# Moving the running sums into the final banks, and the down biases into the twelfth pair, of a mixture-of-experts stage

## The reference

```python
gu = xb @ w_gate_up[e] + b_gate_up[e]                 # 1024 -> 2048
x_glu = jnp.minimum(gu[:, :D_EXPERT], SWIGLU_LIMIT)
x_lin = jnp.clip(gu[:, D_EXPERT:], -SWIGLU_LIMIT, SWIGLU_LIMIT)
act = x_glu * jax.nn.sigmoid(SWIGLU_ALPHA * x_glu) * (x_lin + 1.0)
yr = act @ w_down[e] + b_down[e]                      # 1024 -> 1024
y = segment_sum(yr * gate, token)                     # over the 4 experts of a token
...
x = x + gt2 * rms_norm(y, g_ffn_post)
```

## Time and profile before

| | us |
|---|---|
| median of 3 runs | 1356.5 |
| lowest and highest of them | 1350.71, 1359.32 |
| the profiled execution | 1350.96 |
| its span, first to last instruction | 1349.3 |
| PE busy in it | 1280.7 |
| DVE, ACT busy | 361.6, 218.8 |
| DMA, mean over the span | 365 GB/s |

### The profile page before, as it was taken

How to read it: one execution, slowest core, us unless ns; L and a number is a source line. 1 busy time by engine, 2 the same in 40 slices (tenths; PEclk the granted TensorE clock), 3 DMA queues, 4 the chain that set the end, 5 groups by cost and what they waited for, 6 DMA issues and landing times.

```text
span 1349.3 us, 15432 instructions
## 1 busy us (share of the span) xinstructions
PE 1280.7 (95%) x6118; PEld 542.0 (40%) x6118; DVE 361.6 (27%) x757; ACT 218.8 (16%) x500; POOL 46.7 (3%) x95
## 2 busy tenths in 40 slices
PE   5999999999999999999999999999999999999996
PEld 2566466665453333333233233223423323342322
DVE  2541325776552121111212102121210212121122
ACT  2124424422220111011011011101101101110101
POOL 1100003010100000000000000000000000000000
PEclk9899999999999999999999999999999999999999
DMA  9847569589878999999999999999999999999992
GB/s 347 276 145 286 192 244 254 175 250 292 313 297 349 408 395 431 428 427 426 426 428 428 428 427 428 427 426 427 428 428 428 426 428 428 428 428 428 429 426 106
DMA packets 72718, 492.25 MB, mean 365 GB/s; under 512 B 12229, under 2 KB 25405, under 8 KB 44868
## 3 DMA queue, kind: packets, MB, share of 16 engines
q1 hardware_dynamic: 68708, 480.99, 88.0%
q0 software_dynamic: 3936, 10.21, 2.6%
HBM read 485.86 MB, written 5.32 MB: 364 GB/s over the span
## 4 chain that ended last, share of the span: by engine, by line
PE 72%; DMA 24%; DVE 2%; issue 1%; ACT 0%; SPq 0%; DVEq 0%; ACTq 0%
PE bank L1987 23%; DMA ring<-in_w_gate_up_dram 22%; PE bank L2014 10%; PE bank L1682 8%; PE bank L1709 5%; PE bank L1975 4%; PE bank L1945 4%; PE bank L1548 2%; PE bank L1670 2%; PE bank L1821 2%; PE bank L1622 2%; PE bank L1998 2%; DMA ring<-in_w_down_dram 2%; PE bank L1949 1%; PE bank L1796 1%; PE bank L1978 1%
## 5 line engine op out<-in xcount | busy, mean ns | idle before, releaser
L1987 PE MATMUL bank<-ring,hga 128*64 128x512 f32 x1024 | 236.7, 599 | 13.1 <-DMA ring<-in_w_gate_up_dram 13.1
L1987 PE MATMUL bank<-ring,work 128*64 128x512 f32 x992 | 229.5, 599 | 13.0 <-DMA ring<-in_w_gate_up_dram 9.3
L2014 PE MATMUL bank<-ring,work 128*64 128x512 f32 x1024 | 228.8, 597 | 8.6 <-DMA ring<-in_w_down_dram 8.5
L2014 PEld LDWEIGHTS bank<-ring,work 128*64 128x64 f32 x1024 | 73.1, 138 | 159.2 <-issue 140.6
L1987 PEld LDWEIGHTS bank<-ring,hga 128*64 128x64 f32 x1024 | 67.3, 136 | 158.4 <-issue 129.1
L1987 PEld LDWEIGHTS bank<-ring,work 128*64 128x64 f32 x992 | 65.1, 136 | 153.8 <-issue 127.9
L1459 DVE TENSOR_SCALAR work<-bank 128x512 f32<-128x512 f32 x32 | 22.1, 692 | 351.7 <-PE bank L1987 351.7
L1682 PE MATMUL bank<-hga,ring 128*128 128x320 f32 x384 | 108.1, 443 | 2.2 <-DVE hga L963 2.2
L877 ACT ACTIVATE work<-bank 64x512 f32<-64x512 f32 x60 | 35.5, 591 | 335.7 <-PE bank L2014 335.0
L1682 PEld LDWEIGHTS bank<-hga,ring 128*128 128x128 f32 x384 | 74.1, 194 | 36.8 <-issue 6.6
L1471 DVE TENSOR_TENSOR gbT<-gbT,bank 128x512 f32<-128x512 f32 x80 | 55.0, 687 | 115.4 <-PE bank L1975 80.0
(11 more groups left out here) (368 smaller groups left out, 872.1 us busy)
## 6 DMA issues: line engine op xcount, KB each, us to landing
ring<-in_w_gate_up_dram SPq DMA_DIRECT2D x126, 2048.0 KB, 22.3
ring<-in_w_down_dram SPq DMA_DIRECT2D x64, 2048.0 KB, 23.2
ring<-in_w_ada_dram SPq DMA_DIRECT2D x12, 2048.0 KB, 10.3
ring<-in_w_in_dram SPq DMA_DIRECT2D x12, 2048.0 KB, 11.2
ring<-in_cache_k_dram SPq DMA_DIRECT2D x64, 128.0 KB, 7.2
ring<-in_cache_v_dram SPq DMA_DIRECT2D x16, 512.0 KB, 8.7
ring<-in_w_out_dram SPq DMA_DIRECT2D x2, 2048.0 KB, 9.7
out_dram<-tok POOLq DMA_DIRECT2D x2, 1024.0 KB, 8.4
```

Of the source, the lines that this page charges most:

```text
L1987: last = mm(B[x + 2 * q][CAP * h:CAP * h + CAP, :], slots[:, k, CAP * x:CAP * x + CAP], units[k // 2][:, k % 2, 1024 * q + 512 * h:1024 * ...
L2014: last = mm(B[4 + y][CAP * j:CAP * j + CAP, :], actT[:, 4 * y + m, CAP * h:CAP * h + CAP], slot[:, m, 512 * j:512 * j + 512], start=(h == ...
```

## The change

1. **Last pair.** `summed` for pieces 0, 1, 2 and 3 moves into x = 0, ahead of and between the two halves of `down(t, 0, ...)` (expert 29); piece 4 follows after k = 1 of x = 1. Pair 14 is combined straight on top of them (`combine_ahead`), so its five pieces are no longer added by DVE. `biases` of x = 1 opens the banks ahead of its eight steps. `SUM_BANK` gets other banks; expert 30's down output and the activations of expert 31 go through B[1] for it. `combine_of(0)` is split: pieces 0, 1 and 4 ahead of the last half of `down`, pieces 2 and 3 after it.
2. **Down biases.** They leave the opening. In pair 12 PE turns the gate weights after k = 1 of x = 0 and combines the biases after k = 4, 5 and 6 of x = 0 (`combine_biases`); DVE copies the gate weights (`gates_out`) and adds the five pieces between its two `acts`. On POOL the memsets of `C` and `Ysb` are gone, and b_down is loaded later, behind the wait for `h2tok_made` and ahead of the four loads of `bgu`.
3. **Loops.** `LOOPED = 8`: the hardware loop covers pairs 1 to 8, and pairs 9 to 14 are written out, on every engine.
4. **The end.** DVE's `post_normed` runs in the order 1, 0, 3, 4, 2 and waits for a square only for 0, 4 and 2; ACT's squares of pieces 1 and 3 wait for DVE instead. There is one root instead of two, and the five `y_out` follow it in one go.

```diff
-        SUM_BANK = [B[7], B[0], B[2], B[3], B[6]]
+        SUM_BANK = [B[7], B[6], B[0], B[2], B[5]]
...
-                with eng.Fori(0, (PAIRS - 4) // unroll) as i:
+                with eng.Fori(0, LOOPED // unroll) as i:
...
-                for u in range(1, 3):
-                    pair(t(PAIRS - 4 + u), PAIRS - 4 + u, u)
+                for i in range(LOOPED + 1, PAIRS - 1):
+                    pair(t(i), i, i % 4, i)
...
-            eng.memset(C, 0.0).then_inc(s["moe_zeroed"], 1)
-            eng.memset(Ysb, 0.0).then_inc(s["moe_zeroed"], 1)
-            eng.wait_ge(s["moe_zeroed"], 3)
-            eng.dma_start(Ysb[0:E, :], b_down[0]).then_inc(s["late_in"], 16)
             eng.wait_ge(s["h2tok_made"], 4)
+            eng.dma_start(bd, b_down[0]).then_inc(s["late_in"], 16)
...
             for k, i in enumerate(SUMMED):
                 eng.wait_ge(s["last_ps"], NPC * n + k + 1)
+                if i in (1, 3):
+                    eng.wait_ge(s["u_made"], 5 + (i + 1) // 2 + i // 2)
...
-                if i == 4:
-                    root(r3[:, 0:2], 8)
-            root(r3[:, 2:3], 9)
+            root(r3, 8)
...
+            def gates_out(t):
+                eng.wait_ge(s["wt_ps"], t + PAIRS - BIASED)
+                V_.tensor_copy(cb[:, 0:SP_], B[7][0:E, SP_:2 * SP_]).then_inc(s["wt_made"], PAIRS // 2)
+                V_.tensor_copy(cb[:, SP_:T], B[7][0:E, 0:NS]).then_inc(s["wt_made"], PAIRS // 2)
...
                 acts(t, 0)
                 experts(i)
+                if at == BIASED:
+                    gates_out(t)
+                    for n in range(NPC):
+                        combined(t - 1, n)
                 acts(t, 1)
...
+            for i, last, squared in ((1, 2, 0), (0, 0, 1), (3, 5, 0), (4, 0, 3), (2, 0, 4)):
+                if last:
+                    eng.wait_ge(s["last_ps"], NPC * n + last)
+                if squared:
+                    eng.wait_ge(s["f_sq"], squared)
+                post_normed(i)
...
+                        if at == BIASED and (x, k) == (0, 1):
+                            eng.wait_ge(s["C_made"], t)
+                            weights_turned()
+                        if at == BIASED and x == 0 and k in (4, 5, 6):
+                            combine_biases(t, ((0, 1), (2, 3), (4,))[k - 4])
...
                 for x in range(2):
                     e = 2 * t + x
+                    if x:
+                        biases(t, x, opens=True)
...
-                        gate_up(x, k, slots_of(3), gu_slot)
-                        if x == 1 and k in (1, 2, 3):
-                            if k == 1:
-                                eng.wait_ge(s["C_made"], t + 2)
-                            combine(t, ((0, 1), (2, 3), (4,))[k - 1])
+                        gate_up(x, k, slots_of(3), gu_slot, opened=(x == 1))
+                        if (x, k) == (1, 1):
+                            eng.wait_ge(s["Y_made"], 2 * t)
+                            summed(4)
+                        if x == 1 and k in (2, 3):
+                            combine_ahead(((0, 1, 2), (3, 4))[k - 2])
...
                     if x == 0:
-                        for h in range(2):
-                            down(t, 0, h, dn_slot[h])
-                summed(4)
-                summed(0)
+                        eng.wait_ge(s["C_made"], t + 1)
+                        summed(0)
+                        summed(1)
+                        down(t, 0, 0, dn_slot[0])
+                        eng.wait_ge(s["lin_made"], 4 * t + 1)
+                        summed(2)
+                        summed(3)
+                        down(t, 0, 1, dn_slot[1])
                 down(t, 1, 0, dn_slot[0])
-                acts_turned(2 * t + 2, 1)
-                summed(3)
+                acts_turned(2 * t + 2, 1, B[1])
                 down(t, 1, 1, dn_slot[1])
-                down(t + 1, 0, 0, dn_slot[2])
-                combine_of(0)
-                down(t + 1, 0, 1, dn_slot[3])
-                combine_of(1)
+                down(t + 1, 0, 0, dn_slot[2], B[1])
+                combine_of(0, (0, 1, 4))
+                down(t + 1, 0, 1, dn_slot[3], B[1])
+                combine_of(0, (2, 3))
+                combine_of(1, SUMMED)
```

More of the change, by code:

```diff
@@ L881, in Y_out, with acts @@
                         link.later(ins)
-            def acts(t, x):
+            def acts(t, x, bank=None):
                 y = 1 - x
@@ L919, in last_pair @@
                     eng.wait_ge(s["dn_used"], 4 * t + 2 + 2 * x)
-                    A_(Ysb[:, 512 * x:512 * x + 512], B[4 + x][:, :], ACT.Copy).then_inc(s["Y_made"], 1)
+                    A_(Ysb[:, 512 * x:512 * x + 512], B[1 if x else 4][:, :], ACT.Copy).then_inc(s["Y_made"], 1)
             def again(r):
@@ L1446, in _ @@
             select(4)
[L1447 removed]
+            eng.wait_ge(s["moe_zeroed"], 1)
             def experts(i):
@@ L1507, in again, with post_normed @@
                 select(2 * PAIRS * r + 4)
-            moe_rounds(eng, first, pair, last_pair, first, again)
+            n = moe_rounds(eng, first, pair, last_pair, first, again)
             eng.wait_ge(s["G3_in"], 48)
-            def post_normed(k):
-                i = SUMMED[k]
-                eng.wait_ge(s["f_sq"], k + 1)
-                link.later(TTo(piece(gbf, i).rearrange("p (t n) -> p t n", t=2), SUM_BANK[i][:, :].rearrange("p (t n) -> p t n", t=2),
-                               G3(2 if i == 4 else i % 2), ALU.mult))
+            def post_normed(i):
+                TTo(piece(gbf, i).rearrange("p (t n) -> p t n", t=2), SUM_BANK[i][:, :].rearrange("p (t n) -> p t n", t=2),
+                    G3(2 if i == 4 else i % 2), ALU.mult).then_inc(s["u_made"], 1)
             def y_out(i):
@@ L1988, in gate_up, with biases @@
                                   units[k // 2][:, k % 2, 1024 * q + 512 * h:1024 * q + 512 * h + 512],
-                                  start=(k == 0), stop=(k == NT - 1))
+                                  start=(k == 0 and not opened), stop=(k == NT - 1))
                 if k % 2:
                     last.then_inc(s["gu_used"], 1)
-            def biases(t, x):
+            def biases(t, x, opens=False):
                 eng.wait_ge(s["esel_made"], t + 1)
@@ L1998, in biases, with acts_turned, down @@
                         mm(B[x + 2 * q][CAP * h:CAP * h + CAP, :], esel[E * j:E * j + E, CAP * x:CAP * x + CAP],
-                           bgu[E * j:E * j + E, :], start=False, stop=False)
-            def acts_turned(e, y):
+                           bgu[E * j:E * j + E, :], start=opens, stop=False)
+            def acts_turned(e, y, bank=None):
                 eng.wait_ge(s["act_made"], e)
                 for m in range(4):
-                    last = tr(B[4 + y][:, SL * m:SL * m + SL], glu[:, half_columns(y, m)], 128)
+                    last = tr((bank or B[4 + y])[:, SL * m:SL * m + SL], glu[:, half_columns(y, m)], 128)
                 last.then_inc(s["aT_ps"], 1)
-            def down(t, x, h, slot):
+            def down(t, x, h, slot, bank=None):
                 y = 1 - x
+                bank = bank or B[4 + y]
                 if h == 0:
@@ L2098, in summed, with combine_ahead, combine_of @@
                     mm(SUM_BANK[i][:, :], ident[:, :], piece(gbf, i), start=True, stop=False)
-                def combine_of(x):
-                    eng.wait_ge(s["Y_made"], 2 * t + 2 + x)
-                    for i in SUMMED:
+                def combine_ahead(pieces):
+                    for n in pieces:
+                        i = SCATTER[n]
+                        k = i // 2
+                        if k < 2:
+                            last = mm(SUM_BANK[i][:, :], C[:, 128 * k:128 * k + 128], Ysb[:, 512 * (i % 2):512 * (i % 2) + 512],
+                                      start=False, stop=False)
+                        else:
+                            for h in range(2):
+                                last = mm(SUM_BANK[i][64 * h:64 * h + 64, :], C[:, SP_:T], Ysb[:, 512 * h:512 * h + 512],
+                                          start=False, stop=False)
+                        last.then_inc(s["scatter_ps"], 1)
+                def combine_of(x, of):
+                    eng.wait_ge(s["Y_made"], 2 * t + 1 + x)
+                    for i in of:
                         k, j = i // 2, i % 2
```

124 lines of the change are left out of this document (55 added, 69 removed).

## The result

| | before | changed |
|---|---|---|
| median of the runs, us | 1357.91 (4 runs, 1350.71 to 1359.91) | 1343.85 (4 runs, 1342.12 to 1345.94) |
| ratio, 95% interval | | 0.9915 (0.9886 to 0.9945) |
| the profiled execution, us | 1350.96 | 1342.12 |
| its span | 1349.3 | 1340.3 |

The change saves 0.85%, with an interval of 0.55 to 1.14%. A second set of 7 runs of the changed kernel, beside 12 of the one before, gave 0.9933 (0.9909 to 0.9958). The two medians of the table differ by more, 14.1 us or 1.04%; the ratio on record is not their quotient (0.9896), which lies inside its interval. Forecast was 0.9926, and 1346.5 us with a range of 1341 to 1354.

The account below looks back on a forecast made before the run. PE was taken as the bound to about 510 us, then the weight stream, then PE at the end; 5.4 us (opening), nothing (pair 12) and 4.6 us (end) made 10.0 us, ratio 0.9926, median 1346.5 us, range 1341 to 1354.

Parts of the forecast that it names:

- What bounds the kernel: PE up to about 510 us, then the weight stream, then PE again in x = 1 of the last pair.
- Term 1: Opening: biases and gate-weight transposes leave PE, so the load stream comes 5.4 us earlier (0 to 5.8).
- the last hole: Gap in the load stream at 490 to 510 us, 2.4 us, said to keep its size and come earlier.
- the prediction's own recurrence: Each load lands at the later of its issue plus 7.3 us and the landing before plus 4.9 us.
- rival (a): Only the end gains; the stream is its own bound ahead of 510 us too; 1351.9 us, chance 0.12.
- Term 2: Pair 12 takes the 5.4 us of PE work; later waits absorb it, cost nothing (at most 5.4 us).
- Edits at nothing: POOL's dropped memsets, b_down's later issue and written-out pairs 9 to 12: no effect at the end.
- Terms 3 and 4: Last pair: moved copies and biases fill PE's waits, 2.40 us; two pieces of expert 30 behind the last down, 1.06 us.
- Term 5: Last norm: from ACT's copy to the last product 10.7 us in place of 11.77, 1.1 us less (0 to 2).
- The sum: Whole kernel: opening 5.4 us, pair 12 nothing, end 4.6 us; together 10.0 us, ratio 0.9926.
- The rule on HBM: About 358 GB/s per core, 5.9 us a load, stream the bound from the start, opening's gain nothing; set aside.

Follow-up runs that it names:

- gains_early: Changed kernel with the last norm's gains loaded ahead of the opening and b_down in their place; median 1342.38 us, ratio to before 0.9918.
- end_only: Changed kernel with the down biases back in the opening and not in pair 12; median 1349.13 us, ratio to before 0.9959.
- combine_whole: Changed kernel with all five pieces of expert 30 ahead of the last half of down; 940.47 us from the opening's first matmul to the end.
- after_again: The changed kernel itself run again, nothing altered; median of 7 runs 1345.64 us, ratio to before 0.9933.
- opening_only: Changed kernel with the last pair and the norm as before the change; one run 1357.94 us, 943.63 us from the opening's first matmul to the end.
- gains_twice: Changed kernel with the last norm's gains loaded a second time once the first set has landed; one run, 1347.72 us.
- unrolled_only: Kernel before with only the hardware loop cut to pairs 1 to 8, pairs 9 to 14 written out; 948.34 us from the opening's first matmul to the end.

## Why the prediction was right

The median came out at 1343.85 us, 2.7 below the forecast and inside the range; the ratio is 0.9915 where 0.9926 was forecast. By its steps, counted from O in the traces:

- **What bounds the kernel**: right, and shown by both halves. Work taken from PE in the opening moves the stream; work put into pair 12 or pair 14 doesn't (818.4 to 818.7 us from expert 4's last load to the stream's last, with and without it).
- **Term 1**, 5.4 us: the mechanism is right, the size was too large. By its last landing the stream moved by 4.0 and 3.2 us in the two traces of the changed kernel, and by 3.3 to 4.8 in the four others with the moved biases and the gains in their old place (S has 4.0 and 3.1, and 3.4 to 5.4). What was mis-sized is the sentence that the last hole stays with its size. The 2.4 us came from the windows' bytes; by the prediction's own recurrence the hole was 506.07 - (500.45 + 4.9) = 0.7 us, since the queue was full there up to 500.45. So expert 4's last load could land 5.4 us earlier only if the load before it came 4.7 us earlier, and it came 3.1 to 3.6 us earlier, because the gains stood in front of it. The prediction gives the gains no price. gains_early shows what is left without them: the load before comes 5.8 us earlier, the stream's last load 5.6 to 5.7, S 869.93 - 864.27 = 5.7 us, near the upper bound of 5.8. So rival (a) was right in a part: for 1.5 to 2.5 us the stream was its own bound, by the small loads that it named.
- **Term 2**, nothing: right. No idle time in pair 12, 427 GB/s behind it, PE on time at expert 30; two pairs later it was still nothing.
- **Edits at nothing**: right for the loop. POOL's reordering is in end_only with the biases back in the opening, and there S - O is that of before within 0.2 us.
- **Terms 3 and 4**, 2.40 + 1.06 = 3.46 us: measured 63.39 - 59.34 = 4.05. The waits and the piece were right (combine_whole has its 1.06). Most of the other 0.6 is PE's own work, which takes less time in its new order: from the beginning of x = 1 to the first additions of expert 30 it was 1327.54 - 1290.57 = 36.97 us with five copies, which at 0.96 leave 32.2 for the rest, and now it is 1320.92 - 1288.23 = 32.69 with one, 31.7 for the same rest. It stands there in fewer and longer groups; that this is the reason is not shown.
- **Term 5**, 1.1 us: 1.59. The first square came 1.90 us after the copy where I had kept 2.56, but it is not on the path: the third product waits 0.70 us for PE. PE's last group ended 3.93 us after the copy (forecast 4.25), the last product of the gains 5.89 (forecast 6.2), and the outputs began 0.89 us behind that, where I had 1.1. The five outputs took their 3.4 us.
- **The sum**: 5.4 + 3.46 + 1.1 = 10.0 forecast; 4.0 + 4.05 + 1.59 = 9.6 in the trace, less 0.3 for the last DMAs (3.43 us behind the last product, before 3.16), 9.4. Two misses of opposite sign met, so that the total fits this trace better than its terms do; after_again has 8.4. The ratios of the two sets of runs, 0.9915 and 0.9933, lie on both sides of the forecast 0.9926.

The rule on HBM that I had set aside (the Trainium skill, DMA: Bandwidth & Descriptors, Where 436 GB/s comes from) is not borne out by any trace here: from the sixteenth on the slices of all twelve show 421 to 431 GB/s, for 800 us.

## What to carry to other kernels

Find the last hole in the load stream and ask whose program placed it: work taken from that engine ahead of the hole reaches the end, work moved behind it into the saturated stretch cost nothing here, with 5.2 us of PE's waits for every two pairs to take it up. When the hole closes, the next thing in the queue is the bound, and small loads that were free in a half-empty queue have a price. Where the stages ahead vary by more than the change gives, cut the traces at marks and compare the stretches; here that made effects of 1 us visible under a spread of 11. A mark that hangs on a single load scatters with the stream's pauses, so take the last landing beside it.

## What the runs showed that I had not expected

- The 0.75 MB of gains, issued by GpSimd into a full weight stream, put the loads behind them back by 2.2 to 2.7 us (against gains_early, which has b_down's 128 KB in that place); 0.8 to 2.5 us of it was left at the stream's last load, and with two sets 5.5. Their bytes at 428 GB/s are 1.8 us.
- The opening's first matmul came between 401.05 and 412.47 us in twelve traces, with the same program ahead of it but for POOL's few instructions and loads. This is most of the spread of the runs (before: 1347.18 to 1361.16 us in 19 of them). The traces show where in the mixer it comes from. PE's row of the attention's value product behind its wait, in the kernel before and in opening_only, and the windows of opening_only:

```profile
312.73 1.07 PE L1796 MATMUL bank<-ring,work 128*32 128x256 f32 x16 [0.94 <-issue]
...
320.18 1.94 PE L1798 MATMUL bank<-ring,work 128*32 128x256 f32 x16 [7.56 <-issue]
...
310.00:320.00 10.00, 2.61 (x10) 1.52 (x8) 3.38 (x9) 0.61 (x2) 0.00 (x0) 0.80 1.01 255
320.00:330.00 10.00, 9.82 (x66) 5.03 (x67) 4.74 (x12) 1.19 (x4) 0.00 (x0) 0.52 0.74 175
```

This wait is 0.94 us in the trace of before, the lowest of the twelve, and 7.56 in opening_only, the highest; the six traces with up to 2.4 us have O at 401.05 to 404.86, the five with 3.9 and more at 406.95 to 412.47 (gains_twice, 2.73: 404.20). In opening_only this row is already 7.45 of the 11.42 us late. PE has been idle for 7.56 us there, and the granted clock is down with it: 0.80 between 310 and 320 us and 0.52 between 320 and 330, nearly all of that on the lower level (1.2 of 2.4 GHz), where the trace of before has 1.00 in both. In the code three waits stand there, among them that for the value pages (`v_in`), but the profile puts the idle time down to issue, so what makes it long stays open.
- ACT's first square came 1.8 to 1.9 us after its copy in all traces of the new end, 2.56 in the one before and 1.8 in unrolled_only and opening_only, which have the old end. So the 2.56 belongs to that one trace and not to the order of the work; what it is made of stays open. It didn't decide the old end: unrolled_only has 1.8 and still 11.95 us from copy to last product.
